# Prompt attention of a decoder trunk: values and turns of two query heads of a tile taken together, another order of tiles, a later gather

## The chip, the cores and the metric

The kernel runs on one core of a Trainium2 chip. The metric is the device time of one execution in microseconds (us). TensorE multiplies matrices, VectorE (DVE), ScalarE (ACT) and GpSimd (POOL) do elementwise work, and SP's queue issues most DMA transfers. Each engine works its own instructions in order and waits for the others by semaphores.

## The reference

One layer of a hybrid decoder: normalisation, an input projection, a recurrent branch (RWKV-7) and a sparse attention branch, then a merge. It runs for 1024 prompt tokens and for 8 sample tokens over paged caches of 4096 positions. The part that matters here is the prompt's attention, with 8 query heads of 64 in two key groups `g` of four heads each, and three branches:

```python
s_c = einsum(q, kc) - slope * dist      # 63 compressed keys
p_c = masked_softmax(s_c, c_mask)
s_s = einsum(q, k_g) - slope * s_dist   # selected blocks: with 1024 tokens, all earlier keys
s_w = einsum(q, kw) - slope * w_dist    # window of 512 back
o = g[:, :, 0] * o_c + g[:, :, 1] * o_s + g[:, :, 2] * o_w    # o_x = p_x @ v_x
```

## The kernel before

The kernel is a row of stages, each with its own semaphores and with a barrier of all engines at its end: input projection, recurrent branch, token projection, `attend_prompt`, `compress_sample`, sample attention, merge, output. Only `attend_prompt` and its planner are touched.

**Units.** The 1024 queries are 8 tiles of 128 (`i`), and the heads are taken as `j` = 0 to 3, where head `j` of both key groups `g` goes together, one on the upper and one on the lower 64 rows or columns of TensorE's array. That makes 32 units `n`: `j = n // 8`, tile `AT_ORDER[n % 8]`, so the eight tiles come in the order 0, 4, 7, 1, 6, 2, 5, 3 four times. A unit of tile `i` has, for each `g`, a selected branch (`br` 1) of `i + 1` blocks of 128 keys, a window branch (`br` 2) of `min(i, 4) + 1` blocks, and a compressed branch (`br` 0) of 63 keys. So tile 0 has 3 blocks and tile 7 has 14.

**Steps (S).** Scores are made in steps of at most 512 columns per `g` (`plan.steps`, 88 in all; tile 0 takes one step, tile 7 four). TensorE scores a step into PSUM banks 0 to 3 (two sets; step `s` waits until the mask of step `s - 2` is done). VectorE's `mask` adds distance and mask, takes the row's extreme and writes the scores into SBUF. ScalarE's `exps` takes the exponential in place with the row sum; the exponentials of two steps are issued after those steps, before the copies that follow. Two steps after a unit's last step VectorE caps and inverts its row sums (`coefs`), behind that step's mask in its queue. GpSimd then scales each branch by the inverse and the gate (`scaled`), in the order of branches 1, 2, 0, two instructions (one a `g`) for each.

**Pieces: turns (T) and values (V).** The scaled probabilities are turned on TensorE, a block of 128 at a time, and multiplied with the values. A piece is one PSUM bank of 512 columns: before, two blocks of one unit, for both `g`. Four turns fill bank `4 + pc % 2`; ScalarE (even pieces) or VectorE (odd pieces) copies it to one of five SBUF slots; four value matmuls of 128 columns follow, each of which is two records in the trace. The turn of piece `pc` waits for the copy of piece `pc - 2`. After a unit's last piece VectorE multiplies the output with its gate (`gate`).

**The order** is written out beforehand by `PromptPlan` as a list of events that all engines follow: two steps, then values and turns in twos (VV TT VV TT), where the values are those of the pieces turned in the round before. A round takes 4 pieces from the queue, 5 if it holds more than 8. A unit's pieces join the queue four steps after its last step (`AT_LEAD`). When the steps are over, rounds go on without them (R). The list has 88 steps and 160 pieces.

**Places.** Probabilities lie in a ring `probs` of 6912 columns and in `spare`, 2048 columns of `kT` that are no longer used. The mask of a unit that takes over a place waits for the turns of the unit that had it.

**Gathers.** On GpSimd, before unit `EARLY_CHUNKS`, four indirect DMAs of 1 MB each bring the first cached rows of the next stage into `xnT`, the normalised input, which SP stores to DRAM at the stage's start. `compress_sample` begins with them.

Of the kernel before, what the change touches and what calls it, by code (L numbers as in the profile page):

```python
# [2106 lines left out]
AT_ORDER = (0, 4, 7, 1, 6, 2, 5, 3)  # L2107
AT_SHORT_FIRST = (4, 5, 6)


class PromptPlan:


    def __init__(self):
        self.N = 4 * NT
        self.steps, self.last_step = [], []
        for n in range(self.N):
            i = AT_ORDER[n % NT]
# [19 lines left out]
        self.pieces, self.last_piece, self.first_of = [], [], []  # L2138
# [13 lines left out]
        while ready < self.N or queue or waiting:  # L2152
# [3 lines left out]
        self.place, self.freed, live, at = {}, {}, [], 0  # L2156
        size = AT_RING + 2 * NP
        for n in range(self.N):
            for br in self.by_need(n):
                for g in range(2):  # L2160
                    w = self.width(n, br)
                    if at < AT_RING < at + w:
                        at = AT_RING
                    if at + w > size:
                        at = 0
                    over = [m for m, a, b in live if a < at + w and at < b]
                    self.place[n, br, g] = at
                    self.freed[n, br, g] = max(over) if over else None
                    live = [(m, a, b) for m, a, b in live if not (a < at + w and at < b)] + [(n, at, at + w)]
                    at += w  # L2170
        where = {e: p for p, e in enumerate(self.events)}
        for (n, br, g), m in self.freed.items():
            first = min(s for s, parts in enumerate(self.steps) for part in parts if part[0] == n and part[1] == br)
            assert m is None or where["T", self.last_piece[m]] < where["S", first], (n, br, g, m)

    def turns(self, s, queue, waiting, ready):
        while ready < self.N and self.last_step[ready] + AT_LEAD <= s:
# [6 lines left out]

    def by_need(self, n):
        return sorted((1, 2, 0), key=lambda br: min(s for s, parts in enumerate(self.steps) for q in parts if q[:2] == (n, br)))

    @staticmethod
    def tiles(n, br):
        i = AT_ORDER[n % NT]  # L2190
# [5 lines left out]
    @staticmethod  # L2196
    def first_tile(n, br):
        return max(0, AT_ORDER[n % NT] - 4) if br == 2 else 0

# [17 lines left out]
EARLY_CHUNKS = 16  # L2217
# [16 lines left out]
def attend_prompt(nc, k, x, o):  # L2234
# [3 lines left out]
    with Stage(nc) as ctx:  # L2238
# [4 lines left out]
        spare = k.kT[:, 0:2, :].rearrange("p a n -> p (a n)")  # L2243
# [17 lines left out]
        def region(n, br, g, lo, w):  # L2261
            at = plan.place[n, br, g]
            return spare[:, at - AT_RING + lo:at - AT_RING + lo + w] if at >= AT_RING else probs[:, at + lo:at + lo + w]
# [24 lines left out]
        def _(pe):  # L2288
            def score(s):
# [3 lines left out]
                for n, br, lo, w, first, final in plan.steps[s]:  # L2293
                    j, i = n // NT, AT_ORDER[n % NT]
# [8 lines left out]
            def turn(pc):  # L2303
                n = plan.pieces[pc][0][0]
                pe.wait_ge(scaled, 6 * n + max(2 * (3, 1, 2)[br] for _, br, t in plan.pieces[pc]))
                if pc >= 2:
                    pe.wait_ge(pt_v if pc % 2 else pt_a, (pc - 2) // 2 + 1)
                for b, (n, br, t) in enumerate(plan.pieces[pc]):
                    m = NCMP if br == 0 else P
                    for g in range(2):  # L2310
                        last = nc.tensor.transpose(k.ps[0:m, 4 + pc % 2, (2 * b + g) * P:(2 * b + g + 1) * P],  # L2311
                                                   region(n, br, g, t * P, m), k.ident[:])
                last.then_inc(pt_ps, 1)

            def values(pc):
                n = plan.pieces[pc][0][0]
                if pc == plan.first_of[n] and n >= 2:
                    pe.wait_ge(gatedo, n - 1)
# [1823 lines left out]
```

## Time and profile before

| | |
|---|---|
| median of 3 runs (lowest, highest) | 1679.1 us (1677.68, 1682.85) |
| the profiled execution | 1680.46 us |
| its span | 1678.7 us |
| mean granted TensorE clock | 0.996 of full speed |
| busy over the span: PE, DVE, ACT, POOL | 1624.0, 854.6, 576.9, 396.6 us |
| prompt attention, first score to last value | 668.4 to 911.7 us |
| busy there: PE, DVE, ACT, POOL | 233.6, 167.5, 159.5, 127.7 us of 243.6 |

The profile is of one execution. A row of the timeline gives a start, a length and how many instructions of one form were merged; as TensorE's matmuls are pipelined, a group's price is read from its start to the start of the next group, and not from its length. "L2325" is line 2325 of the kernel: L2298 scores, L2311 turns, L2325 values, L2393 masks, L2352 exponentials, L2403 inverse row sums, L2447 GpSimd's scaling, L2368 and L2424 the copies, L2409 the gate, L2225 the gathers.

### The profile page before, as it was taken

To read this page: it belongs to the slowest core of one execution; us is meant where nothing else is said; L and a number is where in the kernel's file an instruction comes from. 1 tells how busy PE (TensorE), PEld (TensorE's weight loads), DVE (VectorE), ACT (ScalarE), POOL (GpSimd) and SP (SyncE) were. 2 spreads that over 40 slices of the span, in tenths; PEclk is the share of its full clock that TensorE was granted. 3 is DMA by queue.
4 is the path that set the end of the run, shared out by engine and by line. 5 is a ranking of instruction groups with operands and counts; after the bars stand their busy time and mean duration, and the time that the engine had idled before them with its cause. 6 is when DMAs were issued, how large, how long until landed. Compare 5 with 4: busy or idle time off the path is not lost. (4 is left out here: it accounts for less than half of the span.)

```text
span 1678.7 us, 45635 instructions
## 1 busy us (share of the span) xinstructions
PE 1624.0 (97%) x20051; PEld 1163.1 (69%) x20051; DVE 854.6 (51%) x1790; ACT 576.9 (34%) x1244; POOL 396.6 (24%) x455
## 2 busy tenths in 40 slices
PE   8999999999999999999999999999999999999997
PEld 6788777777777555676767889766578888445443
DVE  3433456556555354776776664541152465624344
ACT  5221344454533213666663111223312211102444
POOL 0212223333331130556444220223100032000120
PEclk9999999999999999999999999999999999999999
DMA  5112000100101314712001976468611420700001
GB/s 168 38 50 57 3 17 17 29 17 16 29 17 35 89 32 101 231 74 86 18 2 62 309 286 208 144 144 193 156 26 25 142 60 1 277 0 1 26 25 50
DMA packets 111450, 136.81 MB, mean 82 GB/s; under 512 B 42940, under 2 KB 93829, under 8 KB 106046
## 3 DMA queue, kind: packets, MB, share of 16 engines
q1 hardware_dynamic: 102002, 84.61, 17.3%
q0 software_dynamic: 9216, 49.29, 9.4%
q8 instruction: 159, 2.61, 0.7%
q14 instruction: 37, 0.30, 0.1%
q10 hardware_dynamic: 36, 0.01, 0.0%
HBM read 121.28 MB, written 17.15 MB: 82 GB/s over the span
## 5 line engine op out<-in xcount | busy, mean ns | idle before, releaser
L1265 PE MATMUL ps<-xnT,rw_side_w 64*64 64x344 f32 x2304 | 219.3, 459 | 1.6 <-issue 0.9
L1265 PEld LDWEIGHTS ps<-xnT,rw_side_w 64*64 64x64 f32 x2304 | 98.1, 135 | 33.6 <-issue 12.9
L2733 PE MATMUL ps<-xnT,zT 128*128 128x344 f32 x384 | 120.1, 457 | 0.0
L2447 POOL TENSOR_SCALAR probs<-probs,row_sums,gates 128x63 f32<-128x63 f32 (+6 forms) x148 | 95.6, 662 | 94.8 <-DVE row_sums L2403 94.3
L2733 PEld LDWEIGHTS ps<-xnT,zT 128*128 128x128 f32 x384 | 69.5, 190 | 33.1 <-issue 3.4
L2352 ACT ACTIVATE probs<-probs,neg_max 128x63 f32<-128x63 f32 (+6 forms) x148 | 87.5, 595 | 0.0
L2325 PE MATMUL ps<-probsT,kvtok 128*64 128x128 f32 x1056 | 75.3, 280 | 0.0
L2298 PE MATMUL ps<-kT,zT 64*128 64x512 f32 (+3 forms) x384 | 72.0, 485 | 2.5 <-DVE neg_max L2393 1.6
L2368 ACT ACTIVATE probsT<-ps 128x512 f32<-128x512 f32 (+1 forms) x80 | 45.9, 574 | 82.3 <-PE ps L2311 82.3
L3443 POOL TENSOR_TENSOR mT<-mT,gate_n 128x258 f32<-128x258 f32 x28 | 23.7, 854 | 211.7 <-DVE gate_n L3406 211.7
L2311 PE MATMUL ps<-ident,probs 128*128 128x128 f32 (+1 forms) x460 | 68.1, 279 | 4.8 <-DVE probsT L2424 3.2
L2325 PEld LDWEIGHTS ps<-probsT,kvtok 128*64 128x64 f32 x1056 | 56.0, 136 | 24.0 <-issue 23.0
L2424 DVE COPY probsT<-ps 128x512 f32<-128x512 f32 (+1 forms) x80 | 50.5, 632 | 36.0 <-PE ps L2311 35.1
L1793 POOL TENSOR_TENSOR rw_Lb<-rw_Lm,level_mask 128x512 f32<-128x512 f32 x40 | 54.1, 1360 | 49.7 <-PE ps L1447 33.2
L3342 ACT ACTIVATE zT<-ps 128x258 f32<-128x258 f32 x72 | 27.8, 387 | 107.3 <-PE ps L3324 84.5
L2311 PEld LDWEIGHTS ps<-ident,probs 128*128 128x128 f32 (+1 forms) x460 | 49.8, 140 | 17.6 <-issue 10.2
L3556 PE MATMUL ps<-w_sums,ring_k 128*128 128x512 f32 x128 | 57.2, 593 | 1.4 <-DVE h_tok L3869 1.4
L3324 PE MATMUL ps<-xnT,zT 128*128 128x258 f32 x256 | 57.6, 381 | 0.0
L1003 DVE TENSOR_TENSOR zT<-ps,zT 128x258 f32<-128x258 f32 x30 | 12.8, 426 | 82.5 <-PE ps L868 82.5
L868 PE MATMUL ps<-x_tok,z_sums 128*128 128x258 f32 x240 | 53.8, 381 | 0.0
L3324 PEld LDWEIGHTS ps<-xnT,zT 128*128 128x128 f32 x256 | 48.6, 190 | 7.1
L3869 DVE TENSOR_TENSOR h_tok<-ps,h_tok 128x512 f32<-128x512 f32 x28 | 19.4, 691 | 61.1 <-PE ps L3556 61.1
(625 smaller groups left out, 3584.5 us busy)
## 6 DMA issues: line engine op xcount, KB each, us to landing
w_z<-in_w_in_dram SPq DMA_DIRECT2D x13, 512.0 KB, 5.0
xnT_kept<-xnT SPq DMA_DIRECT2D x1, 4128.0 KB
x_tok<-in_x_prompt_dram SPq DMA_DIRECT2D x8, 512.0 KB
rw_side_w<-in_w_in_dram SPq DMA_DIRECT2D x16, 256.0 KB, 3.3
zT<-in_w_in_dram SPq DMA_DIRECT2D x8, 512.0 KB
ring_k<-in_w_in_dram SPq DMA_DIRECT2D x8, 512.0 KB, 5.3
w_out<-in_w_out_dram SPq DMA_DIRECT2D x1, 4096.0 KB
h_tok<-in_x_prompt_dram SPq DMA_DIRECT2D x8, 512.0 KB, 8.3
```

What stands on the lines that cost most here:

```text
L868: last = nc.tensor.matmul(k.ps[:, bank, 0:cq], left[:, c, :], right[:, c, :], start=(c == 0 and name in ("P1", "P5", "P2")), stop=(c == 3) ...
L1265: last = nc.tensor.matmul(k.ps[half(f), bank, 0:CG], w.side[half(e), g // 3 % 2, c, half(f)], k.xnT[half(e), c, third(g)], start=(phase == ...
L1793: nc.gpsimd.tensor_tensor(w.Lb[:, n % 2], w.Lm[:].rearrange("p q c n -> p (q c) n"), bc(k.tab["level_mask"][:, n + 1, :], 1, 8), ALU.mult) ...
L2298: last = nc.tensor.matmul(k.ps[:, 2 * (s % 2) + g, at:at + w], k.qT[half(g), j, i * P:(i + 1) * P], keys[half(g), t0:t0 + w], start=True, ...
L2311: last = nc.tensor.transpose(k.ps[0:m, 4 + pc % 2, (2 * b + g) * P:(2 * b + g + 1) * P], region(n, br, g, t * P, m), k.ident[:])
L2325: last = nc.tensor.matmul(k.ps[half(g), 6 + n % 2, 0:P], vals, pt[0:m, pc % NPT, (2 * b + g) * P:(2 * b + g + 1) * P], start=(br == 1 and ...
L2352: nc.scalar.activation(every, every, ACT.Exp, scale=-1.0, bias=neg_m[:, at:at + 1], accum_out=ls[:, at:at + 1]).then_inc(expd, 1)
L2424: nc.vector.tensor_copy(to, src).then_inc(pt_v, 1)
L2447: nc.gpsimd.tensor_scalar(every, every, ls[:, at:at + 1], k.gates[:, i, gate:gate + 1], ALU.mult, ALU.mult).then_inc(scaled, 1)
L2733: ins = self.nc.tensor.matmul(self.k.ps[:, self.banks[n % nb], 0:CG], self.w[:, t % 2, c, :], self.k.xnT[:, c, g * CG:(g + 1) * CG], start ...
L3324: last = nc.tensor.matmul(k.ps[:, bank, 0:CQ], stationary(u, n, name, c), moving(u, n, name, c, i), start=(c == 0 and name in ("P1", "P5", ...
L3556: last = nc.tensor.matmul(k.ps[:, bank, :], left[:, c, :], right[:, c, :], start=(first and c == 0), stop=(c == 3), skip_group_check=True)
```

## The change

- Units are numbered anew: `head(n)` is `2 * (n // 16) + n % 2` and `tile(n)` is `AT_ORDER[n // 16][n // 2 % 8]`. So two units that follow each other are heads `j` and `j + 1` of the same tile, a pair `w`; the first eight pairs take the tiles in the order 0, 4, 7, 1, 6, 2, 5, 3, the last eight in the order 7, 4, 6, 5, 3, 2, 1, 0.
- A piece is one block of keys of a pair, for both `g` and both heads. It still takes four turns of 128 columns, and now two value matmuls of 256 columns instead of four of 128. There are 148 pieces. A pair's pieces join the queue four steps after the last step of its second unit. A turn waits for the scaling of its own branch in the pair's second unit.
- One gate instruction covers both heads of a pair.
- The places of probabilities are chosen anew: among free places the one whose last user is oldest, in `probs`, in `spare`, or, for units 4 to 23, in `xnT` too. Masks into `xnT` wait until its store is out.
- The gathers go before unit 26 instead of unit 16, and wait for the last turn that reads from `xnT`.

```diff
-AT_ORDER = (0, 4, 7, 1, 6, 2, 5, 3)
+AT_ORDER = ((0, 4, 7, 1, 6, 2, 5, 3), (7, 4, 6, 5, 3, 2, 1, 0))
+AT_SPARE, AT_INPUT = AT_RING + 2 * NP, AT_RING + 2 * NP + KC * TT
+AT_FIRST_INPUT, AT_LAST_INPUT = 4, 24
...
-        for n in range(self.N):
-            blocks = [(n, br, t) for br in (1, 2, 0) for t in range(self.tiles(n, br))]
+        for w in range(self.N // 2):
             self.first_of.append(len(self.pieces))
-            for a in range(0, len(blocks), 2):
-                self.pieces.append(blocks[a:a + 2])
+            for br in (1, 2, 0):
+                self.pieces += [(w, br, t) for t in range(self.tiles(2 * w, br))]
+                self.last_of[w, br] = len(self.pieces) - 1
             self.last_piece.append(len(self.pieces) - 1)
...
-        while ready < self.N and self.last_step[ready] + AT_LEAD <= s:
+        while ready < self.N // 2 and self.last_step[2 * ready + 1] + AT_LEAD <= s:
...
-EARLY_CHUNKS = 16
+EARLY_CHUNKS = 26
...
             def turn(pc):
-                n = plan.pieces[pc][0][0]
-                pe.wait_ge(scaled, 6 * n + max(2 * (3, 1, 2)[br] for _, br, t in plan.pieces[pc]))
+                w, br, t = plan.pieces[pc]
+                m = NCMP if br == 0 else P
+                pe.wait_ge(scaled, 6 * (2 * w + 1) + 2 * (3, 1, 2)[br])
...
             def values(pc):
...
-                for b, (n, br, t) in enumerate(plan.pieces[pc]):
-                    m = NCMP if br == 0 else P
-                    for g in range(2):
-                        at = (1 + 2 * br) * P + g * HD
-                        vals = k.vc[:, half(g)] if br == 0 else k.kvtok[:, plan.first_tile(n, br) + t, at:at + HD]
-                        last = nc.tensor.matmul(k.ps[half(g), 6 + n % 2, 0:P], vals,
-                                                pt[0:m, pc % NPT, (2 * b + g) * P:(2 * b + g + 1) * P],
-                                                start=(br == 1 and t == 0), stop=(br == 0))
+                for g in range(2):
+                    at = (1 + 2 * br) * P + g * HD
+                    vals = k.vc[:, half(g)] if br == 0 else k.kvtok[:, plan.first_tile(2 * w, br) + t, at:at + HD]
+                    last = nc.tensor.matmul(k.ps[half(g), 6 + w % 2, 0:2 * P], vals, pt[0:m, pc % NPT, 2 * g * P:2 * (g + 1) * P],
+                                            start=(br == 1 and t == 0), stop=(br == 0))
...
                 if n == EARLY_CHUNKS:
                     pool.wait_ge(xn_out, 16)
+                    pool.wait_ge(pt_ps, plan.last_input + 1)
```

## Rows read from the trace of the kernel before

**Rows 1.** The page, busy time of TensorE: us, share of the span, instructions.
```profile
PE 1624.0 (97%) x20051; PEld 1163.1 (69%) x20051; DVE 854.6 (51%) x1790; ACT 576.9 (34%) x1244; POOL 396.6 (24%) x455
```

**Rows 2.** Windows: the stage, its first 16 us, its last 18 us.
```profile
core 0: us, PE busy (x) PEld busy (x) DVE busy (x) ACT busy (x) POOL busy (x), PEclk, DMA share, GB/s
668.30:911.90 243.60, 233.64 (x2292) 164.51 (x2293) 167.51 (x688) 159.46 (x465) 127.71 (x196) 1.00 0.23 75
668.30:684.00 15.70, 12.93 (x104) 7.87 (x106) 12.62 (x61) 12.91 (x35) 6.77 (x12) 1.00 0.97 314
893.80:912.00 18.20, 16.51 (x193) 12.96 (x190) 7.71 (x23) 7.72 (x21) 8.26 (x12) 1.00 0.01 1
```

**Rows 3.** TensorE's timeline, a full round: start us, us, engine, line, operation, count.
```profile
870.22 1.99 PE L2298 MATMUL ps<-kT,zT 64*128 64x512 f32 x8
872.13 1.09 PE L2325 MATMUL ps<-probsT,kvtok 128*64 128x128 f32 x16
873.16 1.09 PE L2311 MATMUL ps<-ident,probs 128*128 128x128 f32 x8
874.18 1.09 PE L2325 MATMUL ps<-probsT,kvtok 128*64 128x128 f32 x16
```

**Rows 4.** TensorE's timeline, four turned pieces in a row, from first to next step.
```profile
883.99 0.33 PE L2311 MATMUL ps<-ident,kT 128*128 128x128 f32 x1
...
886.85 1.99 PE L2298 MATMUL ps<-kT,zT 64*128 64x512 f32 x8
```

**Rows 5.** TensorE's timeline, values that end in compressed rows (x4 more follow).
```profile
883.04 0.66 PE L2325 MATMUL ps<-probsT,kvtok 128*64 128x128 f32 x8
```

**Rows 6.** TensorE's timeline at the start, with idle time and its releaser.
```profile
668.39 0.71 PE L2298 MATMUL ps<-kT,zT 64*128 64x128 f32 x8 [0.95 <-PEq L82]
...
670.58 2.26 PE L2298 MATMUL ps<-kT,zT 64*128 64x512 f32 x8 [0.64 <-DVE neg_max L2393]
...
679.73 1.09 PE L2311 MATMUL ps<-ident,probs 128*128 128x128 f32 x8 [0.47 <-POOL probs L2447]
```

**Rows 7.** TensorE's timeline after the last step, the 18 us tail.
```profile
899.27 0.44 PE L2325 MATMUL ps<-probsT,vc 63*64 63x128 f32 x4
900.96 1.06 PE L2311 MATMUL ps<-ident,probs 128*128 128x128 f32 x8 [1.25 <-DVE probsT L2424]
...
909.68 1.53 PE L2325 MATMUL ps<-probsT,kvtok 128*64 128x128 f32 x24
911.14 0.44 PE L2325 MATMUL ps<-probsT,vc 63*64 63x128 f32 x4
```

**Rows 8.** VectorE's timeline: masks of 512 columns, then an inverse row sum.
```profile
692.81 0.75 DVE L2393 CUSTOM_DVE_ANT_0 kT<-ps,zT,first_min 128x512 f32<-128x512 f32 x1 [0.38 <-PE ps L2298]
...
693.49 0.75 DVE L2393 CUSTOM_DVE_ANT_0 probs<-ps,zT,first_min 128x512 f32<-128x512 f32 x1
...
701.82 0.19 DVE L2403 RECIPROCAL row_sums<-row_sums 128x6 f32<-128x6 f32 x1
```

**Rows 9.** Groups by form, ScalarE in the stage: busy us, mean ns, idle before.
```profile
L2352 ACT ACTIVATE probs<-probs,neg_max 128x640 f32<-128x640 f32 x40 | 32.6, 817 | 0.0
```

**Rows 10.** Groups by form, GpSimd in the stage.
```profile
L2447 POOL TENSOR_SCALAR probs<-probs,row_sums,gates 128x640 f32<-128x640 f32 x40 | 34.8, 882 | 12.8 <-DVE row_sums L2403 12.8
...
L2447 POOL TENSOR_SCALAR probs<-probs,row_sums,gates 128x1024 f32<-128x1024 f32 x8 | 9.5, 1202 | 21.9 <-DVE row_sums L2403 21.9
```

**Rows 11.** GpSimd's timeline at the gathers, and their landing (median us).
```profile
785.82 1.20 POOL L2225 DMA_INDIRECT xnT<-in_cache_k_cmp_dram,chunk_idx  x1 [0.18 <-issue]
...
790.83 2.53 POOL L2447 TENSOR_SCALAR probs<-probs,row_sums,gates 128x128 f32<-128x128 f32 x6
...
xnT<-in_cache_k_cmp_dram,chunk_idx POOLq DMA_INDIRECT x1, 10.5
```

**Rows 12.** Waits in the stage: who, for whom, us in total, times, longest.
```profile
PEld ps L2311 <- POOL probs L2447: 11.7, 26, 1.5
```

**Rows 13.** DMA from 668.3 to 679.5 us: packets, MB, share.
```profile
q1 hardware_dynamic: 127, 4.19, 94.3%
```

**Rows 14.** Groups by form, weight loads of the values.
```profile
L2325 PEld LDWEIGHTS ps<-probsT,kvtok 128*64 128x64 f32 x1056 | 56.0, 136 | 24.0 <-issue 23.0
```

More of the change, by code:

```diff
@@ L2117, in __init__ @@
         for n in range(self.N):
[L2118 removed]
+            i = self.tile(n)
             full, rest = [], []
@@ L2151, in __init__ @@
             queue, waiting, ready = self.turns(s + 1, queue, waiting, ready)
-        while ready < self.N or queue or waiting:
+        while ready < self.N // 2 or queue or waiting:
             self.events.append(("R", len(self.events)))
             queue, waiting, ready = self.turns(len(self.steps) + AT_LEAD, queue, waiting, ready)
-        self.place, self.freed, live, at = {}, {}, [], 0
-        size = AT_RING + 2 * NP
+        where = {e: p for p, e in enumerate(self.events)}
+        self.place, self.freed, taken, self.last_input = {}, {}, [], 0
@@ L2158, in __init__ @@
         for n in range(self.N):
             for br in self.by_need(n):
+                first = where["S", self.first_step(n, br)]
+                last = self.last_of[n // 2, br]
                 for g in range(2):
                     w = self.width(n, br)
[L2162 to L2166, printed above, removed]
+                    held = [q for q in taken if where["T", q[2]] >= first]
+                    at = min(self.room(n, w, held), key=lambda a: (self.newest(a, w, taken), a))
+                    over = [q[2] for q in taken if q[0] < at + w and at < q[1]]
@@ L2167, in __init__ @@
                     self.place[n, br, g] = at
                     self.freed[n, br, g] = max(over) if over else None
[L2169 to L2174, printed above, removed]
+                    taken = [q for q in taken if not (q[0] < at + w and at < q[1])] + [(at, at + w, last)]
@@ new lines, in __init__, with room @@
+                    if at >= AT_SPARE:
+                        self.last_input = max(self.last_input, last)
+    def room(self, n, w, held):
+        zones = [(0, AT_RING), (AT_RING, AT_SPARE)]
+        if AT_FIRST_INPUT <= n < AT_LAST_INPUT:
+            zones.append((AT_SPARE, AT_INPUT))
+        found = []
+        for lo, hi in zones:
+            for at in [lo] + [q[1] for q in held if lo <= q[0] < hi]:
+                if at + w <= hi and not any(q[0] < at + w and at < q[1] for q in held):
+                    found.append(at)
+        return found
@@ L2390, in mask @@
                         elif plan.freed[n, br, g] is not None:
-                            dve.wait_ge(pt_ps, plan.last_piece[plan.freed[n, br, g]] + 1)
+                            dve.wait_ge(pt_ps, plan.freed[n, br, g] + 1)
+                        if first and plan.place[n, br, g] >= AT_SPARE:
+                            dve.wait_ge(xn_out, 16)
                         to = neg_m if final else first_m
```

68 lines of the change are left out of this document (40 added, 28 removed).

## The prediction, made before the changed kernel was run

> **What bounds the kernel now.** I read the page first: TensorE is busy for 97% of the span [rows 1], so what matters is what lies between its matmuls. The windows of the prompt attention come next: it lasts 243.6 us, at the full granted clock, while VectorE is busy 167.5, ScalarE 159.5 and GpSimd 127.7 us; its first 16 us and last 18 us have the most TensorE idle time [rows 2]. So TensorE's order of work sets the end of this stage, which ends at a barrier, and a microsecond there is a microsecond of the kernel. Only this stage is changed.
>
> The timeline of TensorE then prices its three kinds of group. A value group of 16 records takes 872.13 to 873.16, 1.03 us, a turn group of 8 records 1.02 [rows 3], a value group of 24 records 909.68 to 911.14, 1.46 [rows 7]. Eight more value records thus cost 0.43 us: two records, one for each key group, run side by side in 0.109 us. 16 records are 0.87 us of work and 0.15 us for the change of group; a turn is 0.109 us and its group pays 0.15 too. Two scoring steps of 512 columns take 1.91 us [rows 3]: four record pairs of 0.43, and 0.2 for the change. By these prices the stage is 189 us of streaming (592 pairs of value records 64.5, 592 turns of one block 64.5, scores 60), 33 us of changes (43 scoring groups at 0.21, 158 others at 0.15), and the rest, some 22 us, is waiting.
>
> **The change part by part.**
>
> *Values.* 592 record pairs of 128 columns become 296 of 256. The fixed part of a pair is next to nothing: 512 columns cost 0.43, 128 columns 0.109. I take 0.216 for 256 columns, so 296 x 0.216 = 63.9 against 64.5: -0.6 us. Bounds: 0 (all streaming) and, if the 592 weight loads that go each uncovered half a pair's 0.109, -32; the row of 512 columns is the near one.
>
> The Trainium skill ("TensorE: Matmul & The Clock Gate", section on the back-to-back issue gap) speaks otherwise: it gives about 81 ns for a matmul of 128 columns and 131 for one of 512, since the weight load counts in the spacing. By it, wider values would be cheaper by more than a third a column, and some 25 us would go. The trace does not agree: there four times the columns cost four times the time [rows 3, 7].
>
> *Fewer groups.* Written out by the planner's rule (two steps, then values and turns in twos), the order before has 88 steps, 160 pieces and 201 groups; the order after has 88 steps, 148 pieces (a pair of units has 3 to 14 blocks, 74 in each half) and 183 groups: 39 of scores and 144 of the others. 4 x 0.21 + 14 x 0.15 = -2.9 us. The group that goes from full rows to the 63 compressed rows pays 0.15 more: 883.04 to 883.99 is 0.95 us for 12 records, 0.65 + 0.15 + 0.15 [rows 5]. It comes 16 times instead of 32: up to -2.4, I take -2.0 as some coincide with a group's edge.
>
> *Runs of turns.* Only two banks hold turned pieces, so the third turn in a row waits for the copy of the first. Four turns in a row take 883.99 to 886.85, 2.86 us, 0.97 over price [rows 4]. Before there are six such runs and one of three. After, the queue gets a whole pair at once (up to 14 pieces), five go out while it holds more than eight, and where no values wait they go in a row: six runs of five, six of three. A run of three cost 0.6 in the tail; I take 1.2 for five and 0.55 for three: 7.2 + 3.3 - 6.4 = +4.1 us. Bounds -1 (all copies in time) and +9 (each further turn as dear as a copy, 0.69).
>
> *Start.* TensorE waits for VectorE's masks in the first six steps, 2.9 us over price, and values and turns up to 681 lose about 0.7 and 0.9 more [rows 6]. In the new order steps 0 to 11 come with only three turns and three values between, so masks set the pace: a pair of 512-column masks costs 1.36, start to start 0.68 each [rows 8]. Two small steps, six of two units of tile 4 and three steps of 512 and a small one of tile 7 keep VectorE busy until about 685; its reciprocal for unit 3 is behind mask 9, GpSimd's first two scalings (0.88 each, [rows 10]) follow, and the first turn of pair 1 can start at 687.7. The work before it is worth 12.0 us at the prices above, so 7.3 us are idle against 3.6 now (the turns' 0.9 stand in the runs): +3.7. Bounds +1 and +6.
>
> *Lulls.* This is the largest term. A pair's turns are released four steps after its second unit's last step, and so the queue runs empty before pairs 2, 4, 8 and 10 (12 and 14 pieces come after the small tiles 0, 1, 2 or a short queue). Take pair 8, tile 7, whose last step is 51. After it come values 70 to 73 (2.06 us) and steps 52 to 55 with no turn between (about 3.2 us), then turn 74: 5.3 us of work. But turn 74 needs: mask 51 done at +1.5, step 52 only after the values, its mask at +3.8, mask 53 at +5.2, the row sums' reciprocal behind it (VectorE goes in order) at +5.6, then GpSimd's two scalings of 1024 columns at 1.2 each [rows 8, 10]: +8.3. ScalarE's exponentials (0.82 for 640 columns, [rows 9]) are done by +3.5 and hide. So TensorE idles 3.0 us. The same reckoning gives 2.4 us before pair 2, 3.3 before pair 4 (there the masks of 384 columns are ahead) and 2.1 before pair 10. +10.8 us in all. Bounds 0 and +16 (another microsecond and more at each).
>
> *What goes.* Waits for GpSimd at a unit's first turn, 11.7 us over 26 times with the ordinary gaps in them [rows 12]: pairs begin half as often and a turn now needs one branch only. At most half, 5.9, at least 0; I take -3.0. In the tail the 1.3 us wait between 899.27 and 900.96 [rows 7] goes, since small tiles are last: -1.0 (0 to -3).
>
> *The gathers.* Four issues of 0.95 to 1.2 us (785.82 to 790.83, [rows 11]) go from before unit 16 to before unit 26, behind a wait for the last turn that uses the input's place. On GpSimd unit 26's scaling queues behind them. Unit 25's scaling ends 6 us after step 79, the wait (turn 122) is over by then, the issues end at +11; unit 27's first scalings end by about +15 while its first turn comes at about +19: 0 us, and up to +3 if that cover goes. They land 10.5 us after the issue [rows 11], by +25; the stage ends at about +36. Before, they delayed unit 16 by 4 us and TensorE hardly noticed. The new place for probabilities is free once the input's store is out: 4.19 MB have gone by 679.5 [rows 13], its first user is step 10, after 683: 0. Gates (32 of 0.27 to 16 twice as wide), fewer copies and the few extra waits lie on VectorE, which is 69% busy: 0.
>
> Sum: -0.6 - 2.9 - 2.0 + 4.1 + 3.7 + 10.8 - 3.0 - 1.0 = +9.1 us on the profiled execution's 1680.5 (span 1678.7), which is 1.4 over the median of 1679.1. Some of the waits overlap (a run of five that follows a lull finds its banks free), so I take off 0.6: 1679.1 + 8.5 = 1687.6 us.
>
> **The rivals.**
>
> *A, not slower: the waits are absorbed.* One mechanism: the lulls' chain of mask, reciprocal and scaling is shorter than the work TensorE has meanwhile, because VectorE, with no copies to make in a lull, takes each mask as soon as it is scored. Then lulls cost 0, the start 1 and the runs 2.0, which leaves -9.5 + 1 + 2 = -6.5 us: 1672.6. It decides from a chain under 5.3 us at turn 74. For it: VectorE has idle time between masks now. Against: 3.2 us of that chain are GpSimd's two scalings and the reciprocal alone, and today a unit's scaling starts 7 to 9 us after its last step.
>
> *B, faster: the weight loads were the limit.* If the two 64-column loads of a pair, not the columns, set its 0.109 us, halving the loads would give back a part of 64.5 us. For it: the loads are busy 56.0 us for 528 pairs, 0.106 each, as long as a pair takes [rows 14]. Against: the scores stream at the same price a column with far fewer loads. Of the 32 us of the bound above and 0 I take 13, a fifth of the value time: 1679.1 + 8.5 - 13 = about 1675. The skill's rule above would have this come out.
>
> *C, no change.* The lulls cost half (5.4) and the runs 2: 1679.1 - 9.5 + 3.7 + 5.4 + 2 = 1680.7.
>
> *D, much slower.* The gathers land after the stage, or the scaling of unit 26 stands in the way: 1687.6 + 3 to 8, about 1693.
>
> **How the numbers follow.** Forecast 0.53, A 0.10, B 0.07, C 0.20, D 0.10. About 5 us (0.3%) is what a measurement can tell from no change: slower needs over 1684.1, faster under 1674.1. Of the forecast's share 0.50 is slower and 0.03 same; D is slower; A and B split, 0.12 faster and 0.05 same; C is mostly same (0.17; 0.02 faster, 0.01 slower). So slower 0.61, same 0.25, faster 0.14. The range of 8 in 10 goes from between A and C, 1675, to 1695; the forecast's own is 1683 to 1694.
>
> **What would show it.** Value groups of 8 records 128*64 over 256 columns taking 1.01 us: right. Step 55 to turn 74 with some 2 to 3 us of idle TensorE, released by GpSimd, and alike before turns 14, 33 and 99: right; under 1 us there makes rival A. Runs of five turns taking 3.2 to 3.8 us. First turn of pair 1 at 687 to 688. A tail after the last step near 14 us of which under 1 is idle. A stage of about 252 us. It is wrong if the stage is at most 243 us, if value groups are shorter than 0.9 us, or if the next stage starts late by more than this.

## The result and the profile after

The changed kernel took 1698.3 us (median of 7 runs, 1691.03 to 1707.67), the kernel before 1684.8 beside it (7 runs, 1677.68 to 1688.9): a ratio of 1.0085 with a 95% interval of 1.0053 to 1.0118, so 9 to 20 us slower. The forecast was 1687.6 us with a range of 1675 to 1695: the direction was right, the size was not. Of the 10.7 us between 1687.6 and 1698.3, 5.7 are no fault of the reckoning: the kernel before, taken at 1679.1 there, stood at 1684.8 in the comparison. The profiled execution took 1698.47 us with a span of 1696.7, 18.0 over [rows 1]'s kernel.

The page and the windows of the kernel after; the columns of the windows are those of [rows 2].

```profile
span 1696.7 us, 44393 instructions
...
PE 1627.9 (96%) x19459; PEld 1140.3 (67%) x19459; DVE 854.0 (50%) x1768; ACT 576.1 (34%) x1238; POOL 395.5 (23%) x455
```

```profile
670.80:930.10 259.30, 236.14 (x1696) 140.34 (x1696) 166.46 (x665) 158.71 (x459) 127.03 (x196) 0.97 0.22 70
670.80:686.40 15.60, 12.58 (x88) 6.91 (x88) 11.09 (x70) 13.24 (x48) 5.71 (x13) 0.89 1.04 320
805.90:817.30 11.40, 8.89 (x74) 4.94 (x74) 8.58 (x48) 7.76 (x21) 6.55 (x9) 1.00 0.01 2
817.30:820.70 3.40, 3.40 (x16) 2.68 (x15) 0.69 (x1) 1.19 (x2) 2.27 (x4) 0.50 0.00 0
820.70:832.10 11.40, 11.40 (x86) 6.93 (x86) 7.99 (x29) 7.91 (x20) 4.48 (x7) 1.00 0.01 1
912.00:930.30 18.30, 16.86 (x143) 10.73 (x142) 9.21 (x41) 10.58 (x43) 10.35 (x24) 1.00 0.01 2
```

The stage is the first window: 259.3 us against 243.6 [rows 2], so most of the 18.0 lies in it. That window of [rows 2] reaches 0.3 us past the last value, which ends at 911.6. From the first score's start to the last value's end the stage takes 243.2 us before and 259.4 after: +16.2, and these two are compared from here on. It begins 2.4 us later than before, in code that was not changed. VectorE, ScalarE and GpSimd did the same work, within 1.1 us each, while TensorE's busy time rose by 2.5 us although it has less to do. The fourth row shows why: for 3.4 us its granted clock was 0.50. Four such stretches lie in the stage (from 680.8, 694.4, 817.3 and 861.7), none in the stage before, where the granted clock was 1.00 throughout.

TensorE's timeline after, the largest lull, before pair 8's first turn. A row gives start, length, engine, line, operation, count, and the idle time ahead with its releaser. L2324 are scores, L2337 turns, L2350 values, L2474 GpSimd's scaling, L2418 masks, L2426 and L2428 the capping and inverting of row sums, L2450 VectorE's copies, L2375 exponentials, L2391 ScalarE's copies. In the experiments these lines are shifted by up to ten.

```profile
808.78 1.52 PE L2350 MATMUL ps<-probsT,kvtok 128*64 128x256 f32 x12
810.23 0.65 PE L2350 MATMUL ps<-probsT,vc 63*64 63x256 f32 x4
...
813.01 1.13 PE L2324 MATMUL ps<-kT,zT 64*128 64x512 f32 x4 [0.41 <-DVE neg_max L2418]
814.36 0.72 PE L2324 MATMUL ps<-kT,zT 64*128 64x128 f32 x8 [0.21 <-DVE neg_max L2418]
...
817.13 0.33 PE L2337 MATMUL ps<-ident,probs 128*128 128x128 f32 x1 [1.89 <-POOL xnT L2474]
...
817.68 0.42 PE L2337 MATMUL ps<-ident,xnT 128*128 128x128 f32 x1
817.89 0.42 PE L2337 MATMUL ps<-ident,probs 128*128 128x128 f32 x1
```

VectorE and GpSimd in the same lull:

```profile
814.42 0.19 DVE L2428 RECIPROCAL row_sums<-row_sums 128x6 f32<-128x6 f32 x1
...
814.71 1.19 POOL L2474 TENSOR_SCALAR kT<-kT,row_sums,gates 128x1024 f32<-128x1024 f32 x1 [4.85 <-DVE row_sums L2428]
815.88 1.20 POOL L2474 TENSOR_SCALAR xnT<-xnT,row_sums,gates 128x1024 f32<-128x1024 f32 x1
```

Step 51 ends near 808.7. The reciprocal starts 5.7 us later (forecast 5.6), GpSimd's two scalings end 8.4 us after the step (forecast 8.3), and the first turn follows at once: the chain came out as reckoned. What the forecast did not have is in the last two rows. After the wait a turn takes 0.21 us where it takes 0.109 at full clock.

A value group of 8 records and 256 columns, and a run of five turned pieces at full clock (20 turns, 8, 8 and 4 in the rows):

```profile
774.08 1.08 PE L2350 MATMUL ps<-probsT,kvtok 128*64 128x256 f32 x8
775.09 0.33 PE L2337 MATMUL ps<-ident,probs 128*128 128x128 f32 x1
...
779.58 1.09 PE L2337 MATMUL ps<-ident,xnT 128*128 128x128 f32 x8
781.11 1.07 PE L2337 MATMUL ps<-ident,xnT 128*128 128x128 f32 x8 [0.44 <-DVE probsT L2450]
782.61 0.63 PE L2337 MATMUL ps<-ident,xnT 128*128 128x128 f32 x4 [0.44 <-DVE probsT L2450]
783.17 1.13 PE L2324 MATMUL ps<-kT,zT 64*128 64x512 f32 x4
```

The value group takes 1.01 us from start to start. The run takes 3.59 us, and 20 x 0.109 + 0.15 is 2.33: 1.26 over price, where the forecast took 1.2.

A wait that the forecast does not have, first on VectorE, then as the idle time of TensorE that it causes:

```profile
735.65 0.17 DVE L2426 TENSOR_SCALAR row_sums<-row_sums 128x6 f32<-128x6 f32 x1 [1.47 <-ACT probs L2375]
735.96 0.66 DVE L2450 COPY probsT<-ps 128x512 f32<-128x512 f32 x1
...
736.77 1.07 PE L2337 MATMUL ps<-ident,xnT 128*128 128x128 f32 x8 [1.02 <-DVE probsT L2450]
```

VectorE stands for 1.47 us at a unit's row sums, for which ScalarE's exponentials are not done. The copy of a turned piece is next in its queue, and TensorE's next turn needs that copy's bank. This is the wait behind value 27, 1.1 us over price; the same happens behind values 91 and 127, for 1.2 and 0.8 us. A fourth, of 1.5 us behind value 139, looks alike and is not:

```profile
922.11 0.58 ACT L2391 ACTIVATE probsT<-ps 128x512 f32<-128x512 f32 x1
...
922.83 0.30 PE L2337 MATMUL ps<-ident,kT 128*128 128x128 f32 x1 [1.44 <-POOL kT L2474]
```

There the copy that frees the bank is ScalarE's own. It stands behind ScalarE's exponentials and ends at 922.7, at about the same time as GpSimd's scaling, which the row names.

### The profile page after: what moved, and what is told of

It is laid out like the page before. It is cut to its first block and busy times, and to the rows that moved or that the text cites. A ratio compares the mean times of both kernels' runs of the same rounds, so it can differ in the third digit from the quotient of the medians.

```text
span 1696.7 us, 44393 instructions
## 1 busy us (share of the span) xinstructions
PE 1627.9 (96%) x19459; PEld 1140.3 (67%) x19459; DVE 854.0 (50%) x1768; ACT 576.1 (34%) x1238; POOL 395.5 (23%) x455
## 5 line engine op out<-in xcount | busy, mean ns | idle before, releaser
L1265 PEld LDWEIGHTS ps<-xnT,rw_side_w 64*64 64x64 f32 x2304 | 97.9, 133 | 33.5 <-issue 12.1
L2474 POOL TENSOR_SCALAR probs<-probs,row_sums,gates 128x63 f32<-128x63 f32 (+7 forms) x110 | 65.9, 611 | 74.7 <-DVE row_sums L2428 74.7
L2324 PE MATMUL ps<-kT,zT 64*128 64x512 f32 (+3 forms) x384 | 74.0, 497 | 4.7 <-DVE neg_max L2418 3.2
L2391 ACT ACTIVATE probsT<-ps 128x512 f32<-128x512 f32 (+1 forms) x74 | 44.1, 595 | 94.6 <-PE ps L2337 94.6
L2350 PE MATMUL ps<-probsT,kvtok 128*64 128x256 f32 x528 | 73.8, 394 | 0.0
L2450 DVE COPY probsT<-ps 128x512 f32<-128x512 f32 (+1 forms) x74 | 50.7, 686 | 43.5 <-PE ps L2337 43.0
L2337 PE MATMUL ps<-ident,probs 128*128 128x128 f32 (+1 forms) x297 | 54.8, 293 | 6.9 <-POOL probs L2474 2.9
L2375 ACT ACTIVATE probs<-probs,neg_max 128x63 f32<-128x63 f32 (+7 forms) x110 | 60.1, 549 | 1.2 <-DVE neg_max L2418 1.2
L2324 PEld LDWEIGHTS ps<-kT,zT 64*128 64x128 f32 x384 | 32.0, 192 | 32.7 <-issue 19.1
L2474 POOL TENSOR_SCALAR xnT<-xnT,row_sums,gates 128x640 f32<-128x640 f32 (+7 forms) x49 | 38.3, 794 | 63.8 <-DVE row_sums L2428 63.8
L2350 PEld LDWEIGHTS ps<-probsT,kvtok 128*64 128x64 f32 x528 | 31.1, 136 | 30.6 <-issue 21.6
```

The lines of the kernel that those rows point to most:

```text
L1265: last = nc.tensor.matmul(k.ps[half(f), bank, 0:CG], w.side[half(e), g // 3 % 2, c, half(f)], k.xnT[half(e), c, third(g)], start=(phase == ...
L2324: last = nc.tensor.matmul(k.ps[:, 2 * (s % 2) + g, at:at + w], k.qT[half(g), j, i * P:(i + 1) * P], keys[half(g), t0:t0 + w], start=True, ...
L2337: last = nc.tensor.transpose(k.ps[0:m, 4 + pc % 2, (2 * g + jj) * P:(2 * g + jj + 1) * P], region(2 * w + jj, br, g, t * P, m), k.ident[:])
L2350: last = nc.tensor.matmul(k.ps[half(g), 6 + w % 2, 0:2 * P], vals, pt[0:m, pc % NPT, 2 * g * P:2 * (g + 1) * P], start=(br == 1 and t == 0 ...
L2375: nc.scalar.activation(every, every, ACT.Exp, scale=-1.0, bias=neg_m[:, at:at + 1], accum_out=ls[:, at:at + 1]).then_inc(expd, 1)
L2450: nc.vector.tensor_copy(to, src).then_inc(pt_v, 1)
```

## The experiments

The stage's length is from the first score to the last value, in each run's one profile; read from a window it is up to 0.2 us short. The kernel before has 243.2. "Changed kernel" is the kernel after. Each run was compared with runs of the kernel before on the same chip. The ratios compare whole executions, and these differ from the stages by up to 5 or 6 us in either direction: the stage of experiment 3 is 15.9 us longer than before and its time 20.8, the stage of experiment 10 is 1.6 shorter and its time 7.9. So what happens in the stage is read from the stage.

**1. Changed kernel with filler matmuls in its waits (a_filled).** Theory: the clock falls after waits and costs 5 to 7 us; rival: the waits alone cost, and the clock follows them for nothing.

```diff
 def turn(pc):
-    pe.wait_ge(scaled, ...)
     if pc >= 2: ...   # wait for the copy of piece pc - 2
+    if pc in (0, 1, 3, 14, 33, 74, 99): keep_clock(nc, k, 4 + pc % 2, 12)   # 12 matmuls on ident
+    pe.wait_ge(scaled, ...)
 def score(s):
+    if s in (2, 4, 5, 9, 10, 11): keep_clock(nc, k, 7, 6)
```

> The changed kernel with throwaway turns of the identity where TensorE only waits: 12 before the first turn of pairs 0, 1, 2, 4, 8, 10 (1.3 us each, less than the wait there) and 6 before steps 2, 4, 5, 9, 10, 11. Theory (the clock falls because of the waits): the stage shows no stretch at half clock, the mean granted clock returns from 0.992 to 0.995 or more, and the kernel is 5 to 7 us faster than the changed one, so 8 to 10 us slower than before. Rival (the waits alone are the loss and the half clock is incidental): mean clock as in the changed kernel and time within 1 us of it, or 1 to 3 us slower by the fillers.

Measured: 1689.2 us against 1679.9, ratio 1.0057 (1.0038 to 1.0076). Its stage and a later stretch of the same run, then the same lull, then a turn that waited for a copy:

```profile
662.20:918.20 256.00, 244.49 (x1816) 149.10 (x1816) 166.71 (x665) 158.56 (x459) 127.05 (x196) 1.00 0.22 71
1084.50:1111.80 27.30, 27.30 (x175) 21.91 (x175) 24.76 (x13) 3.44 (x6) 0.00 (x0) 0.50 0.01 4
```

```profile
805.97 1.53 PE L111 MATMUL ps<-ident 128*128 128x128 f32 x12
807.93 0.33 PE L2341 MATMUL ps<-ident,probs 128*128 128x128 f32 x1 [0.43 <-POOL xnT L2478]
808.21 0.27 PE L2341 MATMUL ps<-ident,probs 128*128 128x128 f32 x1
```

```profile
772.00 0.33 PE L2341 MATMUL ps<-ident,xnT 128*128 128x128 f32 x1 [0.35 <-DVE probsT L2454]
```

The stage held full clock, no stretch at half was left, and the turns after the lull went at 0.109 us again. The lulls themselves stayed (3.06 and 3.34 us before turns 33 and 74). The nine other runs, of which there is no profile, had a mean granted clock of 0.995 to 0.998, where the changed kernel's thirteen (here and in experiment 5) had 0.987 to 0.995. So in this stage the clock falls because TensorE has nothing to do.

What that costs is less clear. The stage is 3.2 us shorter than the first profile's (256.2 and 259.4, exactly), but the edit did two things. The fillers write the bank of their turn, so the wait for the copy had to come ahead of them, and the two waits changed places for all turns. With that, TensorE stands 0.35 us behind a copy (the last row) where it stood 0.44 in the run shown above: runs of five turns at full clock cost 1.14 over price instead of 1.26, and all such places together some 1.5 us (an estimate from the groups' prices). The fillers also take time: steps 8 to 11 lose 4.4 us over price for 2.9. The clock is thus priced better by rows at either level: in the first profile the runs of turns at 692, 817 and 860, partly or wholly in half-clock stretches, cost 2.2 us more together than the same runs at full clock (1.26 and 1.26 in experiment 5, 1.07 in experiment 9).

The whole execution is 9.6 us over the kernel before by ratio, against 12.1 for the changed kernel without fillers (experiment 5; the intervals overlap). The second row is a stretch in a later stage that the edit does not touch; the profiled run is the slowest of the ten (1702.34 us). In the stage, the larger part of the loss is not the clock.

**2. Changed kernel, turns spread over the steps that they have (a_paced).** Theory: what costs is that pieces leave the queue faster than they come, which gives long runs of turns and then an empty queue; rival: scoring two heads of a tile together delays turns whatever the order.

```diff
-now = queue[:AT_GROUP + (len(queue) > 8)]
+most = AT_GROUP + (len(queue) > 8)
+if ready < self.N // 2:   # rounds until the next pair joins
+    rounds = (self.last_step[2 * ready + 1] + AT_LEAD - s + 1) // 2
+    most = min(most, max(2, -(-len(queue) // rounds)))
+now = queue[:most]
```

> The changed kernel with the queue paced: a round takes as many turns as make the queue last until the next pair's pieces come (2 to 5), so that no round is without turns before pairs 2, 4, 8 and 10. 14 more changes of group (+2.1 us), two runs of five fewer (-2.4). Theory (lulls cost 10.5 us and the clock's falls behind them some 5 more): 10 to 13 us faster than the changed kernel, 2 to 5 slower than before, stage 246 to 249 us, no half clock except perhaps at the start. Rival (the second unit's scaling is the limit wherever the turns stand): the waits move to other turns, within 3 us of the changed kernel.

Measured: 1679.5 us against 1679.9, ratio 0.9992 (0.9964 to 1.0019).

```profile
662.70:908.10 245.40, 231.97 (x1696) 137.50 (x1696) 167.04 (x665) 157.48 (x459) 127.05 (x196) 0.99 0.23 74
```

Six lines of the planner, with no matmul, copy or scaling added or removed, take 13.9 us off the stage (259.3 to 245.4), though the order has 197 groups for 183. The rival falls: with the same units of two heads and one-block pieces the stage is 2.3 us over the kernel before. Four runs of five were left (1.15, 2.01, 1.07 and 1.78 us over price) and two half-clock stretches, one right behind a wait of 1.6 us for a copy that ends at 824.5.

**3. Changed kernel with narrow values (a_narrow).** Theory: wide values bring what their columns say, about 0.6 us; rival B: their loads were the limit, and undoing them costs 13 us.

```diff
-matmul(ps[half(g), 6 + w % 2, 0:2 * P], vals, pt[0:m, ..., 2 * g * P:2 * (g + 1) * P], ...)
+for jj in range(2):
+    matmul(ps[half(g), 6 + w % 2, jj * P:(jj + 1) * P], vals, pt[0:m, ..., (2 * g + jj) * P:...],
+           start=(br == 1 and t == 0 and jj == 0), ...)
```

> The changed kernel with the values again as four matmuls of 128 columns a piece instead of two of 256; everything else stays. Theory (only columns cost): value groups of two pieces take 1.03 us instead of 1.01, 0 to 1.5 us slower than the changed kernel. Rival (weight loads were the limit, so wide values gained): 5 to 13 us slower than the changed kernel.

Measured: 1698.1 us against 1679.9, ratio 1.0124 (1.0083 to 1.0166), stage 259.0 with three half-clock stretches. A value group:

```profile
748.84 1.09 PE L2354 MATMUL ps<-probsT,kvtok 128*64 128x128 f32 x16
749.87 0.33 PE L2337 MATMUL ps<-ident,xnT 128*128 128x128 f32 x1
```

1.03 us with 16 records, 1.01 with 8 wide ones; over the stage the value groups took 83.6 and 83.0 us (82.8 in experiment 5). Rival B falls by these rows: 592 weight loads, taken away or put back, are worth about 0.7 us. The whole executions alone would not have decided it. By ratio this kernel is 20.8 us over the one before, the changed kernel 14.3 and, in experiment 5, 12.1, so 6.5 to 8.7 us more, where the rival expected 5 to 13; the intervals overlap. The stage, 259.1 against 259.4 and 257.4, shows none of that.

**4. Kernel before with the gathers before unit 26 (b_gather26).**

```diff
-EARLY_CHUNKS = 16
+EARLY_CHUNKS = 26
```

> The kernel before with only the gathers moved from unit 16 to unit 26. Theory: they are hidden in either place, within 1 us of before. Rival: behind them GpSimd's scaling of unit 26 comes late or the transfers meet the next stage's, 3 us or more slower.

Measured: 1679.6 us against 1679.9, ratio 1.0008 (0.9985 to 1.0032), stage 244.0. The 0.8 us over 243.2 stand in the first six steps, where 3.4 us from 667.2 ran at half clock, far ahead of the gathers. They cost nothing that can be measured at either place, which takes away rival D's ground. In the kernel after they start at 897.59, and unit 26's scalings follow at 902.60:

```profile
897.59 1.21 POOL L2249 DMA_INDIRECT xnT<-in_cache_k_cmp_dram,chunk_idx  x1 [0.18 <-issue]
...
902.60 0.67 POOL L2474 TENSOR_SCALAR probs<-probs,row_sums,gates 128x384 f32<-128x384 f32 x1
```

**5. The changed kernel once more (a_again).** No edit: how far does the stage vary from run to run?

> The changed kernel once more, for a comparison on the same chip as the three beside it. Theory: stage within 1 us of 259.2, two to five stretches of 3.4 us at half clock in it, 14 to 19 us slower than before (ratio 1.008 to 1.012).

Measured: 1690.7 us against 1678.2, ratio 1.0072 (1.0054 to 1.009).

```profile
663.10:920.40 257.30, 233.02 (x1696) 137.94 (x1696) 166.33 (x665) 158.72 (x459) 127.66 (x196) 0.99 0.22 71
```

The same program has two half-clock stretches here (673.4, 809.9) and four in the first profile, and its stage is 2.0 us shorter. That makes about 1 us a stretch, and some 3 to 4 us of clock in the +16.2 of the first profile, which vary. Counted from the stage's start, the two stretches lie at 10.2 and 146.8 us, where the first profile has two of its four (10.0 and 146.5); experiment 3 has stretches at 10.1 and 146.7 as well.

**6. Paced, and no run of more than one turn beyond the values that wait (a_short_runs).** Theory: runs of five are the rest of the cost; rival: breaking them up adds as many group changes as it saves.

```diff
+most = min(most, len(waiting) + 1)   # after the pacing of experiment 2
```

> The paced kernel, and a round may take at most one turn more than the round before left values: no run of turns is longer than three (seven of three, none of five). Theory (a run of five costs 1.2 us over its price, more after a fall of the clock, one of three 0.55): four runs of five go (-4.8 to -6), five more of three come (+2.8), so 2 to 3 us faster than the paced kernel, stage 242 to 244 us, 1 us faster to 1 us slower than before. Rival (the runs wait for the scaling and not for the copies, so a later start of the pair only moves the wait): within 1 us of the paced kernel.

Measured: 1677.9 us against 1678.2, ratio 1.0002 (0.9981 to 1.0022).

```profile
668.40:911.40 243.00, 229.93 (x1696) 136.76 (x1696) 166.43 (x665) 157.96 (x459) 127.71 (x196) 0.99 0.23 75
```

No run of five is left, seven of three cost 0.53 to 0.60 each (one 1.98), and 2.4 us more went, with one group more. Stage and time are now those of the kernel before (243.2 exactly, both).

**7. The same with fillers in its waits (a_short_filled).** The diff is that of experiment 6, with 8 filler matmuls before turns 0, 1, 3, 33 and 99 and 5 before steps 2, 4, 5 and 11. The two waits of a turn change places here too.

> The kernel with short runs, with 8 throwaway turns before turns 0, 1, 3, 33, 99 and 5 before steps 2, 4, 5, 11, where TensorE waits most. Theory (the clock falls behind such waits): no half clock in the stage, 1 to 3 us faster than the one with short runs. Rival: the fillers only cost, 1 to 3 us slower.

Measured: 1677.0 us against 1678.2, ratio 0.9999 (0.9978 to 1.002), stage 242.3 with no half-clock stretch. Against 243.0 with one: 0.7 us, and the other order of the waits alone is worth about that much by the rows of experiment 1 (an estimate). Fillers bring nothing that can be measured here once the waits are short.

**8. Kernel before, five pieces a round (b_group5).** Theory: long runs cost, whoever makes them; rival: they cost only together with two-head units.

```diff
-now = queue[:AT_GROUP + (len(queue) > 8)]
+now = queue[:5]
```

> The kernel before with rounds of up to five pieces instead of four (five over eight): 13 runs of five turns and 3 of three instead of 6 of four and 1 of three, 194 groups instead of 201, and rounds with one turn or none between. No pairing, no wide values, no other order. Theory (bursts cost, whoever makes them): 13 x 1.2 + 2 x 0.55 - 6 x 0.97 - 7 x 0.15 = +10 us, and as much again if the short rounds leave the first turns waiting for GpSimd: 8 to 16 us slower than before, with half clock now and then in the stage. Rival (the loss of the change lies in pairing itself): within 3 us of before.

Measured: 1696.6 us against 1678.2, ratio 1.0111 (1.0089 to 1.0133). The stage, and one run of five from its first turn to the next step:

```profile
663.60:924.10 260.50, 238.48 (x2288) 165.18 (x2288) 168.85 (x687) 160.41 (x465) 127.05 (x196) 0.99 0.21 70
```

```profile
701.55 0.33 PE L2311 MATMUL ps<-ident,kT 128*128 128x128 f32 x1
...
702.99 0.30 PE L2311 MATMUL ps<-ident,kT 128*128 128x128 f32 x1 [0.34 <-ACT probsT L2368]
...
704.62 0.30 PE L2311 MATMUL ps<-ident,kT 128*128 128x128 f32 x1 [1.00 <-DVE probsT L2424]
...
705.61 1.99 PE L2298 MATMUL ps<-kT,zT 64*128 64x512 f32 x8
```

One number of the planner makes the old kernel as slow as the changed one: +17.4 us in the stage. Thirteen runs of five cost 1.38 to 2.84 us over price, 23.8 together; this one takes 4.06 for 2.33. The releasers are the copies: two banks, 20 turns of 2.18 us, and for each four a copy of 0.60 us on ScalarE or 0.69 on VectorE. The forecast of 10, up to 16, was too low.

**9. Changed kernel, inverse row sums behind the copy (a_late).** Theory: the new waits behind values 27, 91, 127 and 139 come from VectorE standing at a unit's row sums ahead of a copy; rival: TensorE then waits for the later scaling instead.

```diff
 # at a step: only for the units where a lull waits for it
-while done < plan.N and plan.last_step[done] + 2 <= u: coefs(done)
+while done < plan.N and plan.last_step[done] + 2 <= u and (
+        done in (0, 1, 3, 5, 9, 17, 21) or u % 2 == 0 and plan.last_step[done] + 2 < u): coefs(done)
 # after an odd piece's copy
+while done < plan.N and (plan.last_step[done] + 2 <= step or rounds): coefs(done)
 # at a round without steps: all that are left, in the first one all but the last unit's
```

> The changed kernel with VectorE's capping and inverting of row sums moved, except for units 0, 1, 3, 5, 9, 17, 21, from behind the mask to behind the next copy of the round, so that it no longer waits for ScalarE's exponentials ahead of that copy (in the tail only the last unit's moves). Theory (this waiting holds back copies, and with them TensorE, at values 27, 91, 127 and 139 for 1.1, 1.2, 0.75 and 1.5 us over price): 3 to 4.5 us less in the stage, 253 to 256 us, still 9 us or more slower than before. Rival (TensorE then waits for the later scaling instead): within 1 us of the changed kernel.

Measured: 1692.0 us against 1680.2, ratio 1.0069 (1.005 to 1.0087), stage 256.3. The place of the wait shown above, in this kernel:

```profile
731.15 0.65 PE L2350 MATMUL ps<-probsT,vc 63*64 63x256 f32 x4
731.73 1.18 PE L2337 MATMUL ps<-ident,xnT 128*128 128x128 f32 x8
```

```profile
730.24 0.69 DVE L2450 COPY probsT<-ps 128x512 f32<-128x512 f32 x1
...
731.70 0.17 DVE L2426 TENSOR_SCALAR row_sums<-row_sums 128x6 f32<-128x6 f32 x1 [0.77 <-ACT probs L2375]
```

The copy now goes first, VectorE still waits for ScalarE, and TensorE does not. The waits at 27, 91 and 127 are gone, and what the groups of two values lose over price fell by 3.4 us. The one at 139 stayed, where ScalarE's exponentials are late for the copy itself. The theory holds for three of four places, but the total is not told apart from experiment 5 (1.0072), and the stage is only 1.0 shorter than there. Most of what was gained went at the start, where the rival came true:

```profile
681.69 0.19 DVE L2428 RECIPROCAL row_sums<-row_sums 128x6 f32<-128x6 f32 x1
...
687.97 4.58 PE L2337 MATMUL ps<-ident,probs 128*128 128x128 f32 x20 [4.00 <-POOL probs L2478]
```

Unit 2's row sums now wait for a mask two steps later, since no copy comes in between. In experiment 5 this reciprocal starts at 677.51, 14.4 us after the stage's start; here it is 16.6. GpSimd starts later by as much, and TensorE waits 4.00 us for it before pair 1, against 1.48. That first turn comes 1.2 us later in the stage. In two stretches, from 685.0 (within that wait) and from 708.9, 10.2 us ran at half clock, and the two runs of turns there cost 0.9 us more each than in experiment 5.

**10. Experiments 6 and 9 together (a_short_late).**

> The kernel with paced rounds and short runs, with the same move of the inverse row sums. It should keep the gain of the pairs (fewer groups, fewer switches to 63 rows) without lulls, long runs and held copies. Theory: at values 79, 87, 126 and 139 some 4 us over price go, the stage is 239 to 241 us against 243 of before, and the kernel is 2 to 5 us faster than before (ratio 0.997 to 0.999). Rival: the scaling comes later and the same time is waited before first turns, ratio 0.9995 to 1.001.

Measured: 1672.2 us (7 runs, 1666.95 to 1673.51) against 1680.2, ratio 0.9953 (0.9935 to 0.997). It is faster than the kernel before, by 3.0 to 6.5 of 1000.

```profile
661.60:903.00 241.40, 231.41 (x1696) 137.45 (x1696) 167.29 (x665) 157.96 (x459) 127.03 (x196) 0.99 0.24 75
```

Its stage is 1.6 us shorter than that of the kernel before and of experiment 6, which accounts for a fifth of the 7.9 us. The value groups lose 3.6 us less over price than in experiment 6. The start gives about as much back: the wait for GpSimd before turn 3 is 1 us longer, and 6.8 us in two stretches, from 669.8 and 683.5, ran at half clock. The other four fifths are not explained. Between the profiled executions of this kernel and of the one before 12.5 us lie in all, 6.8 of them ahead of the stage and 4.1 behind it, in code that is the same in both. The stage begins at 661.6 here, but at 662 to 664 in experiments 1, 2, 5, 7 and 8 as well, whose times are not low.

## Why the prediction was right in direction and short by seven microseconds

The forecast for the stage was +9.1 us, measured were +16.2. Its terms, each read in the profile after as time over the prices of [rows 3], less the same in the kernel before (they add up to 15.7; the rest is not placed):

| term | forecast | measured |
|---|---|---|
| lulls before pairs 2, 4, 8, 10 | +10.8 | +10.4 |
| runs of turns | +4.1 | +7.0 |
| start | +3.7 | +4.7 |
| wide values, fewer groups | -3.5 | -3.7 |
| what goes: row switches, GpSimd waits, tail | -6.0 | -7.3 |
| new waits for late copies (3.1 on VectorE, 1.5 on ScalarE) | none | +4.6 |

*Lulls: right, place by place.* 2.3, 3.1, 3.3 and 1.7 us against 2.4, 3.3, 3.0 and 2.1. The chain of mask, reciprocal behind it and two scalings held to 0.1 us (814.42 and 817.08). Rival A, by which VectorE would be quick enough, fell; the forecast's own argument against it, that reciprocal and scalings alone are 3.2 us, was the good one. Experiment 2 shows that the lulls hang on the planner's burst and not on two-head units.

*Values and groups: right.* Counts as written out (183 groups, 148 pieces), 1.01 us a value group, 0.7 us for all of the width by experiment 3. (The order before has 42 scoring groups and 159 others, not 43 and 158 as the forecast has it; the -2.9 stays.) The Trainium skill ("TensorE: Matmul & The Clock Gate", section on the back-to-back issue gap) gives sustained spacings that are not in proportion to the columns, 81 ns for 128 and 131 for 512. Here they are in proportion, with 128, 256 and 512 columns at 0.109, 0.216 and 0.43 us, so the measurement decides against using those figures for these fp32 matmuls.

*Gathers: right*, 0 us by experiment 4. Rivals B, C and D fall with these points: the loads are worth 0.7 us, lulls did not halve, and no run shows a loss from the gathers, though the time is beyond D's 1693. (Experiment 4 moved them in the kernel before. In the kernel after, GpSimd has caught up by 909.3, when it stands idle for 2.2 us.)

*Runs of turns: the term was mis-sized.* At full clock the price was right: three runs of five cost 1.07, 1.26 and 1.26 us against 1.2. The other three lie partly or wholly in half-clock stretches and cost 1.77, 1.84 and 2.18, and these 2.2 us are most of the 2.9 that the term is short. The rest is mainly the first run of three, 1.2 us for 0.55. The 1.2 is a price of this order and no rule: in experiment 8 thirteen runs of five cost 1.38 to 2.84, 1.83 on the mean.

*The start: 1.0 short.* The first turn of pair 1 came 21.6 us after the stage's start, against 19.3; 3.4 us from 680.8 ran at half clock.

*The clock: one step that failed.* The prices were taken at "the full granted clock" and nothing in the sum asked whether the lulls that it found would keep it. They did not: each of the four stretches at half clock follows a wait of TensorE, and filling the waits kept the clock at 1.00 in the stage (experiments 1 and 7). It is worth some 3 to 4 us in the first profile, by the difference between the two profiles of this kernel, and half of that in the second. It stands in the runs, 2.2 us, and in the start above.

*The few extra waits: the step that failed by most.* What was to go did go. Outside the runs, the value and turn groups lose 2.7 us less than before even with the new waits, so 7.3 less without them, a little more than forecast. But the forecast took "the few extra waits" on VectorE for nothing because VectorE is 69% busy. That share says nothing of order: an instruction that waits for ScalarE holds up the copy behind it, and TensorE waits for that copy. The waiting itself is not new: in the stage before, VectorE stood for ScalarE at row sums 9 times, 6.3 us in all, and in the one after 6 times, 6.5 us. New is what stands behind it. Three such places cost 3.1 us, and experiment 9 takes them away by moving the instruction. It also shows the other side: moved too far back, the same instruction makes GpSimd late and costs 1.2 us at the start. The fourth wait, 1.5 us behind value 139, is for a copy that stands behind exponentials on ScalarE. It is the 1.4 us of idle time in the tail, where the forecast had under 1. That two large units in succession make ScalarE late at these places, where small and large ones alternated before, is argued from the order and was not tested.

The 2.4 us ahead of the stage are no part of the change: experiments 1 to 10 and both kernels have the stage's start anywhere in 9.2 us. The two comparisons by ratio, +14.3 and +12.1 (1.0085 and 1.0072), stand beside +16.2 and +14.2 in the stage.

## What to carry to other kernels

Two heads of a tile together, one-block pieces and wide values cost nothing in themselves; the loss came from giving the queue a whole pair at once and emptying it greedily. When a change makes units larger, write out how many pieces each round takes until the next unit joins, and spread them over those rounds: one rule for it was worth 14 us of the stage. And an instruction on an engine with time to spare is free only if it never waits with something behind it that the bounding engine needs. Before moving it back, look for what waits for it in turn.

## What the runs showed of the chip

TensorE's granted clock took one of two levels, 1.00 or 0.50 (2.4 and 1.2 GHz). In the profile after, the four of the stage each began within 2 us after a wait of TensorE for GpSimd. Here are two of these waits, and one that no stretch followed:

```profile
692.47 1.09 PE L2337 MATMUL ps<-ident,probs 128*128 128x128 f32 x8 [1.48 <-POOL probs L2474]
694.00 2.64 PE L2337 MATMUL ps<-ident,probs 128*128 128x128 f32 x12 [0.44 <-DVE probsT L2450]
...
748.33 0.33 PE L2337 MATMUL ps<-ident,xnT 128*128 128x128 f32 x1 [1.65 <-POOL probs L2474]
...
860.16 0.33 PE L2337 MATMUL ps<-ident,xnT 128*128 128x128 f32 x1 [1.47 <-POOL probs L2474]
```

Such a wait stood in work that was otherwise dense: in the 11.4 us before 817.3 TensorE was busy for 8.9. At half clock a turn took 0.21 us for 0.109. Two runs of one program had four and two of these stretches. The two of the second run follow the waits before turns 0 and 74, as two of the first run's do; behind the others, as long in the second run as in the first, the clock stayed. So a wait makes a stretch possible and not certain. The Trainium skill ("TensorE: Matmul & The Clock Gate", section on the clock gate, table of the states) gives the same two levels for an idle and a busy TensorE; the trace agrees on the levels.

In three of the ten experiments' profiles (1, 7 and 9) 27.3 us in one piece ran at half clock in a later stage, from 1068.5 or 1084, with TensorE busy throughout (27.30 us, the second row in experiment 1). These profiled runs took 1702.34, 1687.0 and 1702.21 us, 10 to 13 over the medians of their kernels. The kernel before has single runs as far out (1699.99 beside a median of 1680.24), of which there is no profile. Such a stretch is as large as the whole effect under study, so one profiled run is to be read by its stages and never by its total. What brings it stays open.
